# Prompt latent attention: who divides the probabilities by their row sum

## What is computed

```python
# per head h: q, k are (1024, 96), v is (1024, 64)
s = (q @ k.T) * 96 ** -0.5 + causal_mask
p = jax.nn.softmax(s, axis=-1)          # exp(s - max) / sum(exp(s - max))
y_a[h] = p @ v                          # then times silu(gate)
```

## Time and profile before

| | us |
|---|---|
| median of 3 runs | 1917.81 |
| lowest and highest of them | 1917.43, 1931.07 |
| the profiled execution, its own time | 1923.3 |
| its span in the trace | 1921.6 |

### The profile page before, as it was taken

One profiled execution on the slowest core, in us unless ns is written; L12 is line 12 of the kernel. 1 busy time (PEld: TensorE's weight loads), 2 busy tenths in 40 slices (PEclk: granted clock), 3 DMA queues, 4 the chain that ended last, 5 costly groups with the idle time before them and its releaser, 6 DMA issues.

```text
span 1921.6 us, 25291 instructions
## 1 busy us (share of the span) xinstructions
PE 1646.0 (86%) x10102; PEld 1398.2 (73%) x10102; DVE 781.0 (41%) x1424; ACT 510.1 (27%) x963; POOL 33.2 (2%) x61
## 2 busy tenths in 40 slices
PE   6999894269999986788997999989999777886995
PEld 6999892135666654556995999978999745866993
DVE  3222524745555664554216322271222135554215
ACT  2004210514333344442006320110012134321005
POOL 1000000000000000000000100000000100000000
PEclk9999997689999997899999999987999988967997
DMA  4111103010100105063210411010111121003212
GB/s 157 49 44 44 33 12 123 23 33 12 50 1 1 45 1 152 26 193 111 92 58 11 152 47 51 33 35 22 44 55 44 66 99 45 1 6 133 75 36 91
DMA packets 42018, 110.69 MB, mean 58 GB/s; under 512 B 5817, under 2 KB 23402, under 8 KB 40722
## 3 DMA queue, kind: packets, MB, share of 16 engines
q1 hardware_dynamic: 37698, 92.14, 14.6%
q0 software_dynamic: 4240, 17.45, 2.5%
HBM read 96.10 MB, written 13.47 MB: 57 GB/s over the span
## 4 chain that ended last, share of the span: by engine, by line
PE 47%; DVE 6%; ACT 2%; issue 1%; DMA 1%; SPq 0%; POOL 0%; DVEq 0%; ACTq 0%; POOLq 0%
PE ps L518 11%; PE ps L519 11%; PE ps L520 11%; PE ps L1067 2%; PE ps L1178 1%; PE ps L883 1%; PE ps L1807 1%; PE ps L1593 1%; PE ps L788 1%; PE ps L775 1%; PE ps L1459 1%; PE ps L1461 1%; DVE res L1091 1%; PE ps L1203 1%; DVE probs L849 1%
## 5 line engine op out<-in xcount | busy, mean ns | idle before, releaser
L518 PE MATMUL ps<-x_hi,w_hi 128*128 128x352 f32 x1416 | 463.2, 327 | 38.0 <-DVE w_lo L455 25.3
L519 PE MATMUL ps<-x_lo,w_hi 128*128 128x352 f32 x1416 | 458.9, 324 | 0.0
L520 PE MATMUL ps<-x_hi,w_lo 128*128 128x352 f32 x1416 | 458.4, 324 | 0.0
L518 PEld LDWEIGHTS ps<-x_hi,w_hi 128*128 128x128 f32 x1416 | 270.1, 191 | 39.8 <-issue 33.4
L519 PEld LDWEIGHTS ps<-x_lo,w_hi 128*128 128x128 f32 x1416 | 270.4, 191 | 0.1
L520 PEld LDWEIGHTS ps<-x_hi,w_lo 128*128 128x128 f32 x1416 | 269.6, 190 | 0.0
L449 ACT ACTIVATE w_hi<-w_raw 128x1024 fp32r<-128x1024 f32 (+1 forms) x75 | 82.7, 1103 | 499.6 <-PE ps L520 489.0
L518 PE MATMUL ps<-mx_hi,w_hi 128*128 128x352 f32 x480 | 157.1, 327 | 16.6 <-DVE w_lo L455 15.1
L519 PE MATMUL ps<-mx_lo,w_hi 128*128 128x352 f32 x480 | 155.7, 324 | 0.0
L520 PE MATMUL ps<-mx_hi,w_lo 128*128 128x352 f32 x480 | 155.4, 324 | 0.0
L492 DVE COPY z<-ps 128x352 f32 (+1 forms) x90 | 46.8, 524 | 224.5 <-PE ps L520 224.5
(11 more groups left out here) (408 smaller groups left out, 2070.4 us busy)
## 6 DMA issues: line engine op xcount, KB each, us to landing
w_raw<-in_w_in SPq DMA_DIRECT2D x59, 512.0 KB, 3.4
page<-in_cache_mla SPq DMA_DIRECT2D x128, 144.0 KB, 2.7
w_raw<-in_w_out SPq DMA_DIRECT2D x16, 640.0 KB, 4.6
kvs<-in_mem_cache SPq DMA_DIRECT2D x16, 512.0 KB, 8.9
x_res<-in_xT SPq DMA_DIRECT2D x8, 528.0 KB, 3.8
x<-x_next POOLq DMA_DIRECT2D x1, 4224.0 KB, 13.9
x_res<-x SPq DMA_DIRECT2D x8, 528.0 KB, 3.8
out_y<-res POOLq DMA_DIRECT2D x3, 1408.0 KB, 5.9
```

What stands on the lines that cost most here:

```text
L518: pe.matmul(out, w_hi[:, slot, kk], xh[:, k, chunk(c)], start=(k == 0), stop=False)
L519: pe.matmul(out, w_hi[:, slot, kk], xl[:, k, chunk(c)], start=False, stop=False)
L520: mm = pe.matmul(out, w_lo[:, slot, kk], xh[:, k, chunk(c)], start=False, stop=(k == g.k - 1))
```

## The change

The reciprocal stays on VectorE. It now releases a new semaphore, `rc_ready`; VectorE no longer waits for its own step there, and goes on to the maxima. The multiplication of `probs` by it, 64 instructions, one for each unit, goes to GpSimd, which waits for `rc_ready` before each and releases `pn_ready`, for which TensorE's transposes wait as before. On GpSimd they stand between the store of the rotated key and the spill.

```diff
+        rc_ready = sem("rc_ready")
...
             def normalise(n):
                 u = UNITS[n]
                 dve.wait_ge(p_ready, n + 1)
-                v.then(dve.reciprocal(stat[:, 8 + n % 4:9 + n % 4], stat[:, 4 + n % 4:5 + n % 4]))
-                pr = probs_of(n, u)
-                dve.tensor_scalar(pr, pr, stat[:, 8 + n % 4:9 + n % 4], None, ALU.mult).then_inc(pn_ready, 1)
+                dve.reciprocal(stat[:, 8 + n % 4:9 + n % 4], stat[:, 4 + n % 4:5 + n % 4]).then_inc(rc_ready, 1)
...
+        def gp_attention(gp):
+
+            for n, u in enumerate(UNITS):
+                gp.wait_ge(rc_ready, n + 1)
+                pr = probs_of(n, u)
+                gp.tensor_scalar(pr, pr, stat[:, 8 + n % 4:9 + n % 4], None, ALU.mult).then_inc(pn_ready, 1)
...
             gp.dma_start(o["kr"], z[0:32, Z_KR, :]).then_inc(z_out, 16)
+            gp_attention(gp)
             gp.wait_ge(ln_y, KX * NCH)
```

## The result

The changed kernel takes 1998.7 us (median of 4 runs, 1997.09 to 2000.43), the kernel before in the same comparison 1919.83; the ratio is 1.0399 (95% interval 1.0356 to 1.0442). That is 78.9 us between the medians (77 by the ratio), five times the 15 us that were forecast and outside the range. The profiled execution took 1997.09 us, 73.8 more than that of before.

What follows compares the result with a forecast made beforehand. TensorE and the chain feeding it were taken as the bound. Waits of 10.1 + 4.9 + 0.5 us less a 0.5 us gain gave +15 us, so 1933 us for the median; range 1921 to 1962.

Steps and rivals of the forecast that it cites:

- What bounds the kernel: Whole kernel: TensorE, busy 1646.0 of 1921.6 us; a microsecond counts if TensorE or the chain feeding it waits.
- The way in and the way out: Hand-overs from reciprocal to GpSimd and from GpSimd to TensorE's transposes: 0.30 us and 0.10 us a unit.
- The sum's own range: Added time for the whole kernel: +15 us, with +8 to +24 by the bounds of the two ways.
- The multiplication: GpSimd's multiplication: 0.10 us and 1.04 ns a column, from a selection and a memset; 1.16 us for 1024 columns.
- twice the line: GpSimd's multiplication at double the forecast durations: 2.32 us for 1024 columns, 1.26 for 512.
- Where it counts: Three units in each of heads 0 to 5, 10.1 us; long units of heads 6 and 7, 4.9; last unit, 0.5.
- the covered units of 896 columns: Six units in heads 0 to 5: 0.65 us added against 0.99 us of cover, so no cost.
- the last unit: End of the last head: its added 0.45 us counts, as no unit stands behind it.
- The cover of the thirty: The other thirty units of heads 0 to 5: at least 0.99 us of cover against 0.65 added, so no cost.
- The gain on VectorE: Maxima of the next unit start earlier on VectorE: 0.5 us gain booked, bounds 0 and 9.7 us.
- The rival of half the rate: GpSimd multiplies at half the forecast rate in the attention: 43 us more, 1961 us; chance 0.27.
- What follows the attention: Everything after the attention starts 15 us later as a whole and takes as long as before.

Runs made afterwards that it cites:

- the filled kernel: The changed kernel with 73 matmuls whose result nobody reads, put on TensorE ahead of transposes that waited for GpSimd; 1976.2 us, ratio 1.0276 to the kernel before.
- the better change: The kernel before, VectorE multiplying, with each step of rotation moved ahead of the product with the gate; 1913.8 us, ratio 0.9958.

## Why the prediction was wrong, point by point

*What bounds the kernel.* Right. The waits that the prediction read, 18 of 48 units and 15 of 16, are where most of the loss lay: GpSimd on 18 short units of the heads 0 to 5 cost nothing that can be seen, on the 18 that were waited for it cost 45 us. The twelve units of 896 and 768 columns had cover enough only for the duration that was booked.

*The way in and the way out.* Booked 0.30 and 0.10 us; measured 0.09 to 0.10 and 0.05 to 0.06. The 0.29 us before a transfer didn't carry over to an instruction that computes. The page's warning about GpSimd's spans (the Trainium skill, Perfetto Trace Analysis, "GPSIMD Engine Instruction") did not matter here: the span accounted for the whole way but 0.16 us. The sum's own range did not follow from its bounds: with 0.09 to 0.59 us for the two ways instead of 0.40, 27 units give +7 to +20 us, not +8 to +24.

*The multiplication.* This is the term that failed: 0.10 us and 1.04 ns a column, taken from a selection, where it is 0.28 us and 2.50 ns. For 1024 columns 2.84 us against 1.16, and above the upper bound of twice the line, 2.32. The bound was drawn from one row of another operation, and the runs show how far apart operations of the same width are on this engine: 1.04, 1.89 and 2.84 us for copy, product of tensors and product with a scalar. The sentence that a multiplication should be no harder than a selection had no row behind it. The page that was cited for line rate with one input (the Trainium skill, GPSIMD Engine Reference, "Engine selection") does not hold for this operation, which with a constant took 2.51 ns a column, three times the copy's 0.83. The same page's time for a sum of two tensors, by the prediction's estimate 2.2 ns a column, was nearer to the 2.50 measured, though the product of two tensors took 1.67 here.

*Where it counts.* The structure holds with the right number put in. The differences are then 2.14, 1.89, 1.64, 1.39 and 1.13 us for 1024 down to 512 columns (with 0.09 and 0.06 us for the ways): 6 x (2.14 + 1.39 + 1.13) = 28.0, the covered units of 896 columns 6 x (1.89 - 0.99) = 5.4, the last heads 2 x (2.14 + 1.89 + 1.64 + 1.39) = 14.1, the last unit 1.1: 49 us, against 54 measured at the full clock. Of the remaining 5 us the filled kernel tells a part. Its heads 1 to 5 are 30.15 us longer than before, 6.03 a head, where these steps give 4.66 + 0.90 = 5.56. The 0.47 between is mostly the unit of 768 columns: before the change its transposes began 1.27 to 1.41 us behind the multiplication, less than the 1.64 added, so its cover went too, and the next exponentials come 0.34 to 0.47 us later. In the last two heads it is 18.5 us against 15.2; two units of 384 columns, for which nothing was booked, have 0.5 us each of it, and the rest stays open.

*The cover of the thirty.* The 0.99 us held for what was booked and not for what came: twelve more units of the heads 0 to 5 waited, 30 of 48 in all.

*The gain on VectorE.* 32.7 us of work left it in the attention. The exponentials' waits for the maxima went from 9.7 us in 14 to 7.8 in 8, and no gain in time can be seen; 0.5 us was booked. VectorE and GpSimd did not slow each other either, which the prediction had left open: rotation (1246 ns) and the reduction over 1024 columns (1224 and 1225 ns) last as long after the change as before.

*What was left out.* The clock. The prediction had no term and no rival for it, and it was worth 22 us, more than the whole forecast of 15. That longer waits would leave TensorE idle was in the sum; that the matmuls between them would then be slower was not. Before the change the clock was 1.00 over an attention in which TensorE was busy 93% of the time by the record (261.46 of 282.50); after it, 83% and 0.89.

*The rival of half the rate* was the right mechanism with 43 us at 2.08 ns a column; with the measured durations and ways it is 49, and the clock, which it did not have either, most of the rest. It had a chance of 0.27, and the forecast 0.58.

*What follows the attention* started later as a whole and was as long as before, 1198 against 1201 us. Right.

## What to carry to other kernels

Before an instruction moves to GpSimd, its own duration has to be seen there; another operation of the same width says little, and here a product with a scalar was the slowest of the three operations measured. What counts is not whether the engine that loses the work was busy, but what waits for that instruction: the same move cost nothing that can be seen in 18 units and 45 us in 18 others. A wait that is added to TensorE's feed can have two prices, the wait and the clock of what is computed around it; here the second, 22 us, was two fifths of the first, 54. A step that stands ahead of an awaited instruction may find room where its engine waits anyway; here that was the better change.

## What the runs showed of the hardware

- On GpSimd, float32 over 128 partitions in place: copy 0.30 us for 128 and 1.04 us for 1024 columns, product of two tensors (one of them one column, broadcast) 0.40 and 1.89 us, product with a column or a constant 0.60 and 2.84, or 0.53 and 2.78 us. Each repeated within 17 ns.
- VectorE to GpSimd 0.09 to 0.10 us, GpSimd to TensorE 0.05 to 0.06 us, for instructions that compute. An engine more in the chain was cheap; what it did there wasn't.
- With TensorE idle for 61 instead of 21 us of the attention the granted clock went from 1.00 to 0.89, and 73 matmuls whose result nobody reads, put into the waits, brought it back to 1.00 and the kernel down by 22.5 us.
